# The head norm of a differential attention: statistics of 128x4 spread by a second matmul, or of 128x512 from the start

## The reference, cut to what matters

```python
def rmsnorm(x, g):
    xf = x.astype(jnp.float32)
    y = xf * lax.rsqrt(jnp.mean(xf * xf, axis=-1, keepdims=True) + EPS)
    return (y * g.astype(jnp.float32)).astype(x.dtype)

def differential_attention(h, w_qkv, w_o, ...):
    ...
        attn = probs[:, :, 0] - lam * probs[:, :, 1]
        return jnp.einsum('bhqk,bkhe->bqhe', attn.astype(v.dtype), v)
    ...
    o = o.transpose(1, 0, 2, 3, 4).reshape(B, T, HEADS_B, 2 * HEAD_DIM)
    o = rmsnorm(o, subln_g) * (1.0 - lambda_init)
    return o.reshape(B, T, D_MODEL) @ w_o
```

## Time and profile before

| | |
|---|---|
| median of 3 executions | 1660.09 us (1659.3 to 1660.87) |
| the profiled execution | 1661.8 us, span 1660.0 us |
| busy, share of the span | PE 98%, DVE 56%, ACT 37%, POOL 4% |
| mean granted clock of TensorE | 0.993 of full speed |
| loop of the second mixer, steps 2 to 8 | about 1030 to 1200 us of the span |

### The profile page before, as it was taken

The page is one execution under the profiler, slowest core; times in us unless marked ns, Lnnn a source line. Parts: engine busy times, 40 slices in busy tenths (PEclk is TensorE's granted clock), DMA queues, the critical chain, the costliest instruction groups (busy, mean ns, idle before and its releaser), DMA issues.

```text
span 1660.0 us, 22157 instructions
## 1 busy us (share of the span) xinstructions
PE 1625.1 (98%) x8285; PEld 1331.0 (80%) x8285; DVE 928.2 (56%) x1625; ACT 609.7 (37%) x1053; POOL 70.4 (4%) x66
## 2 busy tenths in 40 slices
PE   7999999999999899999999999999989999999997
PEld 5888888888888678888888878888868888888885
DVE  6454554554555663545445676777686354545554
ACT  5234234243243432222223444665553222222343
POOL 2000000000000200000001110000020000000111
PEclk8999999999999999999999999999999999999998
DMA  5543343342332233333333332323223333333331
GB/s 147 138 122 96 102 130 86 100 132 81 88 96 69 61 101 95 96 101 88 101 89 101 106 111 77 90 62 98 61 71 101 102 89 101 94 99 97 91 110 67
DMA packets 308312, 159.66 MB, mean 96 GB/s; under 512 B 31156, under 2 KB 303085, under 8 KB 308254
## 3 DMA queue, kind: packets, MB, share of 16 engines
q1 hardware_dynamic: 308254, 158.88, 33.9%
HBM read 156.64 MB, written 10.60 MB: 101 GB/s over the span
## 4 chain that ended last, share of the span: by engine, by line
PE 93%; DVE 4%; ACT 1%; DMA 0%; SPq 0%; issue 0%; POOL 0%; ACTq 0%
PE unit_out L1314 27%; PE unit_out L1316 27%; PE unit_out L1315 27%; PE turned L1390 2%; PE attn L1443 2%; DVE act_lo L968 1%; PE attn L1651 1%; PE logits L1314 1%; PE logits L1390 1%; PE misc L1390 1%; DVE rstd L973 1%; DVE heads L1140 1%; PE logits L1316 1%; PE logits L1425 1%; PE logits L1315 1%; ACT w_hi L740 0%
## 5 line engine op out<-in xcount | busy, mean ns | idle before, releaser
L1314 PE MATMUL unit_out<-act_hi,w_hi 128*128 128x512 f32 x2024 | 804.6, 398 | 11.6 <-DVE act_lo L968 9.8
L1316 PE MATMUL unit_out<-act_hi,w_lo 128*128 128x512 f32 x2024 | 789.4, 390 | 0.0
L1315 PE MATMUL unit_out<-act_lo,w_hi 128*128 128x512 f32 x2024 | 788.9, 390 | 0.0
L1314 PEld LDWEIGHTS unit_out<-act_hi,w_hi 128*128 128x128 f32 x2024 | 380.9, 188 | 102.4 <-DVE act_lo L968 12.4
L1316 PEld LDWEIGHTS unit_out<-act_hi,w_lo 128*128 128x128 f32 x2024 | 380.3, 188 | 80.8
L1315 PEld LDWEIGHTS unit_out<-act_lo,w_hi 128*128 128x128 f32 x2024 | 380.7, 188 | 77.7 <-issue 2.4
L740 ACT ACTIVATE w_hi<-w_raw 128x1024 fp32r<-128x1024 f32 (+3 forms) x259 | 274.1, 1058 | 437.2 <-PE unit_out L1316 360.7
L953 DVE TENSOR_TENSOR w_lo<-w_raw,w_hi 128x1024 fp32r<-128x1024 f32 (+3 forms) x259 | 324.0, 1251 | 102.4 <-ACT w_hi L740 102.3
L725 POOL TENSOR_TENSOR sumsq<-sumsq,square 128x512 f32<-128x512 f32 x49 | 68.3, 1394 | 1578.1 <-ACT square L758 1576.3
L851 ACT ACTIVATE act_hi<-hidden 128x512 fp32r<-128x512 f32 x64 | 40.5, 633 | 243.2 <-DVE hidden L1159 243.2
L1156 DVE TENSOR_TENSOR scaled<-unit_out,rstd 128x512 f32<-128x512 f32 x64 | 44.2, 690 | 67.7 <-PE unit_out L1316 67.6
(11 more groups left out here) (203 smaller groups left out, 1154.5 us busy)
## 6 DMA issues: line engine op xcount, KB each, us to landing
w_raw<-in_w_ff_dram SPq DMA_DIRECT2D x128, 512.0 KB, 4.0
w_raw<-in_a_w_qkv_dram SPq DMA_DIRECT2D x72, 512.0 KB, 3.9
w_raw<-in_b_w_qkv_dram SPq DMA_DIRECT2D x24, 512.0 KB, 5.1
w_raw<-in_w_ple_gate_dram SPq DMA_DIRECT2D x16, 512.0 KB, 4.0
bias_tiles_b<-bias_vectors SPq DMA_DIRECT2D x16, 256.0 KB, 4.3
bias<-bias_tiles_b SPq DMA_DIRECT2D x8, 512.0 KB, 3.9
w_raw<-in_a_w_o_dram SPq DMA_DIRECT2D x8, 448.0 KB, 3.6
w_raw<-in_b_w_o_dram SPq DMA_DIRECT2D x8, 384.0 KB, 3.5
```

The lines of the kernel that those rows point to most:

```text
L1314: te.matmul(bank, w_k[0], hi, start=start, stop=False)
L1315: te.matmul(bank, w_k[0], lo, start=False, stop=False)
L1316: return te.matmul(bank, w_k[1], hi, start=False, stop=stop)
```

## The change

Both kernels start from `square[1]`, the squares of a head's output. Before, four matmuls with the squares as weights and one column of ones give the sums as 128x4 (tokens on the partitions), root, reciprocal and test are of that small shape, four multiplications with `ident` put the factors on diagonals (`square[0]`, 128x512), and a fifth matmul with a full matrix of ones brings each token's factor to all partitions. After, one matmul with the full matrix of ones gives each token's sum on all partitions at once. Root, reciprocal and test are of 128x512, in place in `square[0]`, and the head is scaled by `square[0]` in place of the bank `misc`.

```diff
--- before.py
+++ after.py
@@ -271,8 +271,6 @@
         fold = sb("fold", [P, SUB])
         quarter = sb("quarter", [P, NT])
         spare = sb("spare", [P, 1])
-        head_root = sb("head_root", [P, NT])
-        head_rstd = sb("head_rstd", [P, 2, NT])
         end_col = sb("end_col", [P, NT])
         end_scale = sb("end_scale", [P, NT])
 
@@ -475,8 +473,6 @@
         o_clamped = sem("o_clamped")
         orstd_kept = sem("orstd_kept")
         oss_ps = sem("oss_ps")
-        diagonals_ready = sem("diagonals_ready")
-        spread_ps = sem("spread_ps")
         oroot_ready = sem("oroot_ready")
         orstd_ready = sem("orstd_ready")
         o_normed = sem("o_normed")
@@ -920,7 +916,7 @@
                                   ).then_inc(osq_ready, 1)
                 if has_norm and i == norm_at:
                     wait(sc, oss_ps, s - 1)
-                    sc.activation(head_root[:, :], misc[:, 0:NT], ACT.Sqrt, scale=1.0 / P,
+                    sc.activation(square[0][:, :], misc[:, :], ACT.Sqrt, scale=1.0 / P,
                                   bias=eps_col[:, 1:2]).then_inc(oroot_ready, 1)
 
                     sc.activation(spare[:, :], eps_col[:, 0:1], ACT.Exp)
@@ -1262,19 +1258,13 @@
                 if has_norm and i == norm_at:
 
                     wait(ve, oroot_ready, s - 1)
-                    ve.reciprocal(head_rstd[:, 0, :], head_root[:, :]).then_inc(orstd_ready, 1)
+                    ve.reciprocal(square[0][:, :], square[0][:, :]).then_inc(orstd_ready, 1)
                     wait(ve, orstd_ready, s - 1)
-                    ve.scalar_tensor_tensor(head_rstd[:, 1, :], misc[:, 0:NT], OVERFLOW,
-                                            head_rstd[:, 0, :], ALU.is_lt, ALU.mult
-                                            ).then_inc(orstd_kept, 1)
+                    ve.scalar_tensor_tensor(square[0][:, :], misc[:, :], OVERFLOW, square[0][:, :],
+                                            ALU.is_lt, ALU.mult).then_inc(orstd_kept, 1)
+                if has_norm and i == norm_at + 1:
                     wait(ve, orstd_kept, s - 1)
-                    for a in range(NT):
-                        last = ve.tensor_scalar(square[0][:, a * P:(a + 1) * P], ident[:, :],
-                                                head_rstd[:, 1, a:a + 1], None, ALU.mult)
-                    last.then_inc(diagonals_ready, 1)
-                if has_norm and i == norm_at + 1:
-                    wait(ve, spread_ps, s - 1)
-                    ve.tensor_tensor(hidden[:, :], scaled[:, :], misc[:, :], ALU.mult
+                    ve.tensor_tensor(hidden[:, :], scaled[:, :], square[0][:, :], ALU.mult
                                      ).then_inc(o_normed, 1)
                     wait(ve, o_hi_ready, s + (A_PAIRS - 1))
                     ve.scalar_tensor_tensor(MID[1][1][:, bass.ds((s - 2).v, 1), :], flat3(hidden),
@@ -1580,10 +1570,8 @@
                 if has_scores:
                     wait(te, v_ready, s + GROUPS * A_PAIRS)
                 wait(te, osq_ready, s - 1)
-                for a in range(NT):
-                    last = te.matmul(misc[:, a:a + 1], square[1][:, a * P:(a + 1) * P], ones[:, 0:1],
-                                     start=True, stop=True)
-                last.then_inc(oss_ps, 1)
+                te.matmul(misc[:, :], ones[:, :], square[1][:, :], start=True, stop=True
+                          ).then_inc(oss_ps, 1)
 
             def sub_b(s, par, i, has_proj, has_scores, has_prev, has_norm):
                 u = s.times(B_UNITS) + U_B
@@ -1609,11 +1597,6 @@
                     wait(te, probs_ready, t)
                     turn(turned, [(c * P, probs[prev % 2][:, c * P:(c + 1) * P])
                                   for c in range(prev_q + 1)]).then_inc(turned_ready, 1)
-                if has_norm and i == (3 if has_scores else 2):
-
-                    wait(te, diagonals_ready, s - 1)
-                    te.matmul(misc[:, :], ones[:, :], square[0][:, :], start=True, stop=True
-                              ).then_inc(spread_ps, 1)
                 if has_proj:
 
                     first = s.reg is None and s.const == 0
```

## The result

| | before | changed |
|---|---|---|
| median | 1660.26 us (4 runs, 1659.3 to 1660.87) | 1674.34 us (4 runs, 1672.28 to 1677.6) |
| ratio | | 1.0081, 95% interval 1.0064 to 1.0099 |
| profiled execution, span | 1661.8, 1660.0 | 1672.28, 1670.4 |
| mean granted clock, profiled | 0.993 | 0.993 |
| mean granted clock, the other runs shown | | 0.990, 0.991, 0.990 |

The change makes the kernel slower by 0.8%. In the profiled executions it is 10.4 us of span; between the medians it is 14 us. The two differ by 3.6 us: the profiled execution of the kernel before is 1.5 us over its kernel's median, and that of the changed kernel 2.1 us under its own. The changed kernel's other executions also have a lower mean clock than the profiled one.

What follows compares the result with a forecast made beforehand. PE's own work was taken to set the step; after the change a 26.95 us chain through DVE would. Five steps added 8.6 us, the end 1.3: 9.9 on the span, 1670.0 us at the median, range 1667 to 1674.

Steps and rivals of the forecast that it cites:

- PE's saving: On PE, narrow matmuls go and one wide matmul replaces another: 0.81 us less per head; 6.9 us in all with diagonals' wait.
- DVE's and ACT's durations: In the norm, reciprocal 3.35 us, reciprocal and test together 4.00 on DVE; root 0.69 in place of 0.26 on ACT.
- the two estimates: For the 128x512 reciprocal on DVE, from the skill page: 0.53 us as a plain stream, 4.27 at 8 cycles per result.
- the second estimate: Reciprocal on DVE at 8 cycles per result, 4.27 us: the change would cost some 7 us more than forecast.
- The chain: From slot 1's turn to the next step's, over ACT, DVE and SP: 26.95 us, step 1.71 longer, 8.6 over five steps.
- SP's issue of the bias load, with the weights' load behind it, to ACT's `w_hi`: Chain piece over the load, 5.82 us; its route 7.5 us, as good as equal to DVE's own route of 7.4.
- The 1.9 us at which the kernel was to come out even: Duration of the wide reciprocal on DVE at which the kernel would be neither faster nor slower.
- PE waiting about 2 us before slot 1's turn: Sign in the trace: this PE wait in five steps of 26.9 us, with some tenths more around slot 0's turn and product.
- The last steps: Mixer's end, steps 7 to 9: waits of 3.2 and 0.9 us less savings of 2.4 and 0.4, adding 1.3 us.
- The wait for `act_lo` of step 7: PE at the output product's first unit in step 8: a wait of 3.2 us, where there was none.
- the wait for `w_lo` in step 9: PE wants it at about 1213.9 but DVE has it ready at 1214.8: 0.9 us of waiting.
- the rival that I gave 0.03: The clock falls behind PE's waits: 6 us of each of six steps at 1.2 GHz, 3 us each, 1688 us; chance 0.03.

Runs made afterwards that it cites:

- experiment 1: Changed kernel with its wide reciprocal taken over only 128x4 elements, root and test staying wide: 1653.97 us, ratio 0.9956 to the kernel before.
- experiment 8: Changed kernel with root and reciprocal made by one ACT instruction on 128x512, squares' scale and clamp adjusted: 1653.71 us, ratio 0.9951 to the kernel before.
- experiment 4: Changed kernel with the bias tile's load one place later in SP's queue, behind unit 1's weights: 1674.81 us, ratio 1.0075 to the kernel before.
- experiment 3: Kernel before with one more 128x512 reciprocal on DVE, right behind the four diagonals: 1671.93 us, ratio 1.0062 to the kernel before.
- experiment 2: Changed kernel with its reciprocal over the first 256 of 512 columns: 1659.93 us, ratio 0.9985 to the kernel before.
- experiment 7: Changed kernel with root's reciprocal and the test moved from slot 2 to behind slot 3's key split: 1696.98 us, ratio 1.0206 to the kernel before.
- experiment 5: The changed kernel itself run again, nothing altered: 1674.64 us, ratio 1.0076 to the kernel before.
- experiment 6: Changed kernel with DVE's evacuation of unit 1 ahead of the wide reciprocal in slot 2: 1667.15 us, ratio 1.0039 to the kernel before.

## Why the prediction was right, point by point

The direction and the mechanism were right, and the chain's sum was close. The time was 4.3 us under the measured median of 1674.34, which lies 0.3 us over the upper end of 1674; by the ratio, 1.0081, it is 1673.5 us and within. Of the 4.3 us, 0.5 stand in the profiles (10.4 us of span for 9.9), and 3.6 between profiles and medians, as said with the result; 0.2 us are the kernel before, whose median came out at 1660.26. That the profiles agree to 0.5 us is in part luck, as the sum below shows.

**PE's saving: right.** 0.81 us of a step were forecast. Experiments 1 and 8 have steps of 24.34 and 24.35, 0.90 under 25.24. Both run 7.7 to 7.9 us under the kernel before, where 6.9 were forecast. The saving was mis-sized by a tenth of a us a head: the stretch that held the removed wide matmul became 0.95 shorter (12.63 to 11.68, above) and not 0.8, and the new one, with 0.86 for 0.8, made its own 0.07 longer.

**DVE's and ACT's durations: right.** Reciprocal 3352 ns where 3.35 was forecast, from reciprocal to evacuation 4.00 (1095.20 to 1099.20) where 4.00 was, root 688 ns where 0.69 was. The Trainium skill, "VectorE: DVE Perf Modes", section "Walkthrough: the 8-slice pipeline in each mode", gives one result per cycle for a plain operation and a repeat count of 8 for the reciprocal. The eight new instructions bear out neither of the two estimates worked out from that, 0.53 and 4.27 us: 3352 ns is between them. The row of the same shape was the price. (By the second estimate the prediction has "some 7 us more"; with 0.92 us in five steps and twice in the last ones it is 6.4.)

**The chain: right in kind, 0.20 us too long, and in part another one.** The step is 26.75 where 26.95 was forecast. The piece that failed is "SP's issue of the bias load, with the weights' load behind it, to ACT's `w_hi`": it was forecast to be as good as equal to DVE's own route, and experiment 4 shows that without it nothing is gained, to 0.01 us in a step. From slot 3's first scores to slot 0's exponential the sum had 7.50 us, and the trace has 7.31 (1099.80 to 1107.11); all other pieces came out within 0.03. DVE's own list binds: from reciprocal over the scores and both splits of slot 3, the scaling of the head, `act_lo` and the evacuation of unit 2 to slot 0's scores. That this chain is what costs is shown by experiment 1 (its longest member gone, the wait gone), 3 (the member alone, the wait back), and 2, where half of it closes almost all of the slack and costs little. The 1.9 us at which the kernel was to come out even fit that: with 1.75 us the ratio is 0.9985.

**Where PE waits: half wrong.** I looked for "PE waiting about 2 us before slot 1's turn" and some tenths at slot 0. It is the other way round: 1.75 us at slot 0's scores and 0.49 at the turn. Slot 0's scores need the low part of the keys, which DVE makes at the end of slot 3 (L959, at 1102.20), and this wait (`qk_ready`) was missing from my list. It changed the sum by nothing, since PE has to be at slot 1's turn by DVE's time in any case. But it put the long wait into slot 0, where a fall of the clock behind it costs 1.0 us; behind the long wait at the turn, in experiment 7, it cost 2.5 to 2.8.

**The last steps: 1.8 where 1.3 was forecast.** The wait for `act_lo` of step 7 came in two pieces, 1.68 at the scores and 1.14 at the first output unit, 2.8 for 3.2; the wait for `w_lo` in step 9 was 1.06 for 0.9; and 0.38 at the last turn had been counted at nothing. That is 4.3 us of waiting for 4.1; the other 0.3 us are saving that did not come (2.5 us from step 7's turn to the end, for 2.8), and were not traced to a place.

**The sum on the profile: right in size, in part by luck.** From first to last turn of the loop the changed kernel takes 134.84 us and the kernel before 126.21: 8.6 more, as forecast, but made of 5 x 1.51 and one fall of the clock of 1.05. The steps were forecast 1.0 us too long together, and a fall that the sum didn't have made up for it. With the 1.8 of the end this is the 10.4 us of span, against 9.9.

**The clock: the rival that I gave 0.03 is part of the result, but not at its price.** Falls behind PE's new waits are shown: behind the waits of 1.75 us at slot 0's scores in 6 of 15 steps (one of five in the first trace of the changed kernel, two in experiment 5's, three in experiment 4's), at 1.0 us each, and once in three traces behind the pair of waits in step 8, at 2.6 us. Each trace of the changed kernel thus has 1 to 4.6 us of them. Two things point to them as what lies between profile and median: the first trace had the fewest of the three, and experiment 3, with steps as long and no fall in its trace, is 2.9 us faster than experiment 4 on the same chip. It isn't shown for the unprofiled executions: their mean clocks of 0.990 and 0.991 don't say where the clock was low, in experiment 5 the runs with the lower mean are not the slower ones, and 1.5 of the 3.6 us come from the profiled execution of the kernel before. So the share of the clock in the last 3.6 us stays open.

What I had against this rival, 2.45 us of idle time in a stretch at the mixer's end with the clock at 1.00, was one case and not a rule: behind the same wait of 2.1 us there (2.06 in the kernel before) the clock stayed up in most traces and fell in those of experiments 2 and 5. Falls came behind waits of 1.75 us in some steps and behind 2.33 in all of them; none came behind the waits of 0.88 and 1.16 in the loops of experiments 3 and 6. The Trainium skill, "TensorE: Matmul & The Clock Gate", Part 1, has the clock follow PE's recent work. The trace agrees in kind, with the clock at 0.63 and 0.50 behind these waits; why equal waits of 1.75 us had a fall in 6 steps and none in 9 no run here shows. The price that I had put on it, 3 us in each of six steps, was near that of the seventh experiment and not that of this kernel.

## What to carry to other kernels

An engine that is busy for 56% can still carry the bound: lay the chain through its list around the loop once, with start-to-start times, and compare it with the busiest engine's period, before and after. Here the slack was 1.5 us in a step by the sum (1.7 by the measured step, 26.75 less the 3.2 by which DVE came later, against 25.24), and an instruction of 3.35 us on the idle engine turned a saving of 0.9 us on the busy one into a loss. Look through the list of waits of the engine that will stand still for all that hangs on the late part, since a long wait can cost more than its own length, through the clock, and most where no later wait takes up the rest. And where an operation is wide only because that saves a broadcast, price it by a row of the same shape: a reciprocal of 128x512 took 3.35 us where a multiplication of that shape takes 0.68.

## What the runs showed of the hardware

- Behind a wait of 1.75 us of PE in a loop that is otherwise full, at slot 0's scores, the granted clock fell to 1.2 GHz in 6 steps of 15 (steps of 27.8 among steps of 26.75), and behind 2.33 us, with a wait of 0.96 about 4 us earlier, in every step. A fall cost 1.0 us where a later wait took the rest, and 2.5 to 2.8 us where none did (experiment 7, and step 8 in experiment 5).
- A run's mean clock also depends on the first 45 us of the program, which had 0.89 in one trace and 0.96 in another. The runs of the kernel before on one chip (1659.97 to 1664.74 us, clocks of 0.993 to 0.996) are mostly the slower ones at the lower mean, but there are runs at 0.994 both at 1661.69 and at 1664.74; in experiment 5 the order is the other way round.
- A reciprocal on DVE took 178 ns for 128x4, 1752 for 128x256 and 3352 for 128x512: 6.25 ns for each further element of a partition.
- The reciprocal root of 128x512 on ACT takes 690 ns, no more than the root.
